# Moving eight modulation chunks of the second layer into the first layer's second attention

## The chip, the cores and the metric

The kernel runs on one core of one Trainium2 chip. The metric is the time of one execution on the device in microseconds, as the median of several runs. A profiled execution gives the trace that is read here. Engines are named as in the profile: PE is TensorE (PEld its weight loads), DVE is VectorE, ACT is ScalarE, POOL is GpSimd, SP is SyncE, whose queue (SPq) issues the weight loads.

## What is computed

The reference is a backbone of two layers (`DEPTH = 2`) over 256 latent tokens and 256 context tokens of width 1024, all in float32. Cut to what matters here:

```
for l in range(DEPTH):
    mod  = sc  @ w_mod[l] + b_mod[l]            # six vectors of 1024 for the latent tokens
    modc = scc @ w_mod[l] + b_mod[l]            # and six for the context tokens
    sh1, s1, g1, sh2, s2, g2 = split(mod)
    h = modulate(x, norm1_g[l], sh1, s1)        # needs vectors 0 and 1 (chunks 0 to 3)
    y, yc = token_mixers(h, hc, ...)            # conformer, Hyena, two attentions, gates, w_out
    x = x + g1 * y                              # vector 2 (chunks 4 and 5)
    h2 = modulate(x, norm2_g[l], sh2, s2)       # vectors 3 and 4 (chunks 6 to 9)
    x = x + g2 * hier_moe(h2, ...)              # vector 5 (chunks 10 and 11); 16 experts
```

`sc` and `scc` come from the conditioning vectors alone, so the modulation of the second layer can be computed at any time. In the second layer the context tokens are only keys and values, so most of its steps handle half as many tokens.

## The kernel before, in words

**The order.** The whole program is a list of steps written by hand in `layer_order` (L256): each is a pair of an engine (T for PE, V for DVE, S for ACT, P for POOL) and a name such as `("gate", l, branch, j)`. Every engine runs its own steps strictly in the order of the list and waits by semaphores for what a step needs. `spread` (L178) lays one list of groups evenly among another; `settled` (L192) moves the attention's output products behind the next gate step.

**A modulation chunk** (`mod_steps`, L208) is 512 of the 6144 columns of `w_mod`, and four steps: `mod` on PE (L1011 to L1021, matmuls on L1019, reading a chunk of 2 MB from the weight ring), `modrow` on ACT (L1541, a copy out of PSUM), `modT` on PE (transposes, L1025) and `modcol` on DVE (L2035, a sum and the bias). There are twelve chunks for each layer. For the second layer, chunks 0 to 3 are computed in the first layer's first attention (`ahead`, L342), chunks 4 and 5 at the layer boundary (L389 to L391) and chunks 6 to 11 between the projections of the second layer (L281 to L288, `mods`).

**The ring of weights.** All weights but those of the odd experts go through three places of 2 MB (`RING = 3`). `plan_ring` (L426) walks the chunks in the order in which PE first uses them and gives each the place whose present chunk is last used earliest. SP (L890 to L976) issues the loads in that same order on one queue: for each it waits until the last step that reads the place's earlier chunk is done, then issues the load. A load that waits holds back all loads behind it.

**Around the first layer's second attention (attention C).** `gate_groups(0, False)` is eight pairs of a `gate` step (L1059, 16 matmul records) and a `br` step (L1157), laid between the scores (`sC`, L1186), the transposes of the weights (`pTC`, L1193) and the outputs (`yC`, L1229). Gates 0 to 3 read chunk `("win", 0, 6)`, gates 4 to 7 `("win", 0, 7)`, the eight `br` steps `("wbr", 0, 0)`. Then come the gates of branch 2, which read `("win", 0, 10)`, `("wbr", 0, 2)` and `("win", 0, 11)`.

**The boundary of the layers.** The experts of the first layer end on PE (L1357); ACT stores the last rows to `y_dram` (L1774 to L1778); POOL gathers each token's two results (L1876) once the stores have landed and PE and ACT have ended their expert steps (L1866 to L1872); `mix` (L1248, L1249) adds them on PE, DVE gates them and adds them to `x` (L2579, L2583), then norm and `hT` (L1040) lead to the second layer's projections. At L963 to L965 SP waits for the last gather before it loads `("win", 1, 0)`, the second layer's first projection weights.

**The second layer's projections** on PE in order, with the chunks 6 to 11 (`mod`, then `modT` one or two steps later) between them: four `zD` and six `zB` (L1059), `zC` 0 and 1 (L1069), `vxT` (L1125), `zC` 2, four `dft` (L1131), `lnmean` (L1117), `zC` 3, `lnvar`, two `idft` (L1141), and `zAq`, `zAk` (L1069). Beside them DVE runs the convolutions in its own order: `cfconv` (L2112), `hyconv` (L2089 to L2093), `vx`, then `xc` (L2147) behind `lnmean` and `spec` (L2173 to L2178), for which `idft` waits.

Of the kernel before, what the change touches and what calls it, by code (L numbers as in the profile page):

```python
# [28 lines left out]
DEPTH = 2  # L29
# [108 lines left out]
def live(l):  # L138

    return TILES if l < DEPTH - 1 else 2  # L140


def with_side(l):

    return live(l) == TILES
# [32 lines left out]
def spread(main, side):  # L178

    out, n = [], 0  # L180
    for i, g in enumerate(main):
        upto = (i + 1) * len(side) // len(main)
        out += [g] + side[n:upto]
        n = upto
    return out
# [6 lines left out]
def settled(groups):  # L192

    groups, i = list(groups), 1
    while i < len(groups):
        kinds = [g[0][1][0] for g in groups]
        if kinds[i] in ("yA", "yC") and kinds[i - 1] in ("pTA", "pTC"):
            j = i + 1
            while j < len(groups) and kinds[j] not in ("gate", "br", "pTA", "pTC", "yM"):
                j += 1  # L200
            if j < len(groups) and kinds[j] in ("gate", "br"):
                groups.insert(j, groups.pop(i))
                i = j
        i += 1
    return [s for g in groups for s in g]


def mod_steps(l, chunks):  # L208
    out = []
    for c in chunks:  # L210
        out += [("T", ("mod", l, c)), ("S", ("modrow", l, c))]
        out += [("T", ("modT", l, c)), ("V", ("modcol", l, c))]
    return out
# [13 lines left out]
def filter_groups(l):  # L227

    net = [[("T", ("hf", l, n)), ("V", ("hfarg", l, n)), ("S", ("hfsin", l, n))] for n in (1, 2, 3)]
    net += [[("T", ("hf4", l, i)), ("V", ("hfwin", l, i)), ("S", ("hfsq", l, i))] for i in range(2)]  # L230
    spectrum = [[("T", ("fnorm", l)), ("V", ("fnorms", l))]]
    spectrum += [[("T", ("fdft", l, m)), ("S", ("fdftout", l, m))] for m in range(4)]
    return net, spectrum


def norm_steps(l, n, tiles):

    out = [("S", ("sq", l, n, t)) for t in tiles]
    out += [("V", ("rstd", l, n, tiles[0], tiles[-1] + 1))]
    out += [("V", ("scale", l, n, t)) for t in tiles]  # L240
    return out


def modulated_half(l, n, half):

    out = [("V", ("modfin", l, n, half))]
    for k in range(4 * half, 4 * half + 4):
        out += [("T", ("hT", l, n, k)), ("V" if k % 2 else "S", ("hTout", l, n, k))]
    return out


def modulated_steps(l, n):
    return modulated_half(l, n, 0) + modulated_half(l, n, 1)


def layer_order(l):  # L256

    tt = live(l)
    mods = [mod_steps(l, [c]) for c in range(4, 12)]
    pads = [("V", ("pads", l)), ("S", ("lamexp", l)), ("V", ("lam", l))]  # L260
    if l == 0:
        net, spectrum = filter_groups(l)
        first = [mod_steps(l, [c]) for c in range(4)]
        squares, normed = norm_steps(l, 1, range(TILES))[:TILES], norm_steps(l, 1, range(TILES))[TILES:]
        o = pads + net[0] + first[0][:2] + net[1] + first[0][2:] + squares[:2] + net[2] + squares[2:] + normed
        o += first[2][:2] + net[3] + first[2][2:] + modulated_half(l, 1, 0) + net[4]
        o += [("T", ("zD", l, 2))] + first[1][:2] + [("T", ("zD", l, 0))] + spectrum[0] + first[1][2:]
        o += [("T", ("zD", l, 3))] + first[3][:2] + spectrum[1] + [("T", ("zD", l, 1))] + spectrum[2] + first[3][2:]
        o += modulated_half(l, 1, 1) + spectrum[3] + spectrum[4]
    else:  # L270
        o = norm_steps(l, 1, range(TILES)) + modulated_steps(l, 1) + pads
        mods[:2] = [], []

    zd = {j: [("T", ("zD" if l else "zDrest", l, j)), ("S" if j >= 2 else "V", ("zDout", l, j))] for j in range(4)}
    zb = [[("T", ("zB", l, j)), ("S", ("zBout", l, j))] for j in range(6)]
# [18 lines left out]
    def gate_groups(bi, first):  # L294
        out = []
        for j in range(KD):
            out += [[("T", ("gate", l, bi, j)), ("S", ("gtanh", l, bi, j))],
                    [("T", ("br", l, bi, j)), ("V", ("gmul", l, bi, j))]
                    + ([] if first else [("P", ("gadd", l, bi, j))])]
        return out  # L300
# [17 lines left out]
    def attention(b):  # L318
        units = [(t, h) for t in range(tt) for h in HEADS_OF[b]]
        groups, turn = [], []  # L320
        for i in range(len(units) + 2):
            group = []
            if i < len(units) and i % 2 == 0:
                group += [("T", ("s" + b, l, t, h, n)) for t, h in units[i:i + 2] for n in range(2 if b == "A" else 1)]
            if i < len(units):
                group += [("V", ("mx" + b, l, *units[i])), ("S", ("ex" + b, l, *units[i]))]
            if 1 <= i <= len(units):
                group += [("V", ("p" + b, l, *units[i - 1]))]
            groups += [group] if group else []
            if i >= 2:  # L330
                t, h = units[i - 2]
                groups += turn[:1]
                turn = turn[1:]
                groups += [[("T", ("pT" + b, l, t, h)), ("S", ("pTout" + b, l, t, h))]]
                if h == 3 and b == "C":
                    groups += [[("T", ("yC", l, t)), ("S", ("yToutC", l, t))]]
                elif h == 3:
                    groups += [[("T", ("yA", l, t)), ("S", ("ysqA", l, t))]]
                    turn = [[("T", ("yM", l, t)), ("V", ("yrA", l, t))], [("T", ("yR", l, t)), ("V", ("ynA", l, t))]]
        return groups + turn  # L340

    ahead = []  # L342
    for c in range(4 if l + 1 < DEPTH else 0):
        steps = mod_steps(l + 1, [c])
# [5 lines left out]
    ropes = [[("V", ("rsC", l))]] + [g for g in prepared("C") if g[0][0] == "V"]  # L350
    o += settled(spread(conformer[12:] + spread(gate_groups(1, False), ahead),
                        units[:half] + spread(units[half:], ropes) + turns))
    o += settled(spread(gate_groups(0, False), attention("C")))
    net, spectrum = filter_groups(l + 1) if l + 1 < DEPTH else ([], [])

    o += merge(gate_groups(2, False), net)
# [29 lines left out]
    o += [("V", ("rows", l))]  # L386
    o += [("T", ("experts", l)), ("S", ("experts", l)), ("V", ("experts", l)), ("P", ("experts", l))]
    o += [("V", ("diag", l))] if with_side(l) else []
    if l + 1 < DEPTH:  # L389
        one, two = mod_steps(l + 1, [4]), mod_steps(l + 1, [5])  # L390
        o += one[:2] + two[:2] + one[2:] + two[2:]  # L391
    for t in range(tt):
        for hf in range(2):
            o += [("T", ("mix", l, t, hf))] if with_side(l) else []
# [24 lines left out]


ORDER = [("S", ("silu", 0))] + [s for l in range(DEPTH) for s in layer_order(l)]
STEPS = {e: [n for x, n in ORDER if x == e] for e in "TVSP"}
COUNT = {e: {n: i + 1 for i, n in enumerate(STEPS[e])} for e in "TVSP"}
# [106 lines left out]
def build_trunk(nc, xin, ccol, const, cols, rows, hfw, wr, wmod, win, wbr, wout, w1, w3, w2, out):  # L530
    with ExitStack() as ctx:
# [3 lines left out]
        def sem(name):  # L535
            return ctx.enter_context(nc.semaphore(name))
# [215 lines left out]
        y_gathered = [sem(f"y_gathered{t}") for t in range(TILES)]  # L752
# [96 lines left out]
        def _(sp):  # L849
# [40 lines left out]
            for i, (name, _) in enumerate(CHUNKS):  # L890
# [10 lines left out]
                if name[0] in experts_weights:  # L901
                    l = name[1]
# [57 lines left out]
                                    sp.wait_ge(more_stored[l], b * (16 * NE) + e * 16 + 16)  # L960
                                sp.sem_inc(waited, 1)
                    continue
                if name == ("win", 1, 0):  # L963

                    sp.wait_ge(y_gathered[live(0) - 1], 32)  # L965
                src = source[name[0]][name[1], name[2]]
                width = src.shape[1]
                if name[0] == "win" and name[2] in (2, 3):
# [1717 lines left out]
```

## Time and profile before

| | |
|---|---|
| median of 3 runs | 1601.78 us (1601.4 to 1606.16) |
| the profiled execution, its own time | 1604.79 us |
| its span in the trace | 1603.1 us |
| PE busy | 1491.4 us (93%) |
| DVE, ACT, POOL busy | 598.5, 288.9, 93.4 us |
| mean granted clock of TensorE | 0.972 of full speed |
| moved by DMA | 354.53 MB, 221 GB/s in the mean |

The profiled execution lies 3 us above the median. Times in the rows are microseconds from the start of the span. A timeline row gives start, length, engine, line, operation, what it writes and reads, and in brackets how long the engine stood idle before it and what released it. Records of successive matmuls overlap by some 0.15 us, so what a step takes of PE is read from the start of one row to the start of the next.

### The profile page before, as it was taken

To read this page: it belongs to the slowest core of one execution; us is meant where nothing else is said; L and a number is where in the kernel's file an instruction comes from. 1 tells how busy PE (TensorE), PEld (TensorE's weight loads), DVE (VectorE), ACT (ScalarE), POOL (GpSimd) and SP (SyncE) were. 2 spreads that over 40 slices of the span, in tenths; PEclk is the share of its full clock that TensorE was granted. 3 is DMA by queue.
4 is the path that set the end of the run, shared out by engine and by line. 5 is a ranking of instruction groups with operands and counts; after the bars stand their busy time and mean duration, and the time that the engine had idled before them with its cause. 6 is when DMAs were issued, how large, how long until landed. Compare 5 with 4: busy or idle time off the path is not lost.

```text
span 1603.1 us, 17603 instructions
## 1 busy us (share of the span) xinstructions
PE 1491.4 (93%) x6666; PEld 748.4 (47%) x6666; DVE 598.5 (37%) x1502; ACT 288.9 (18%) x596; POOL 93.4 (6%) x107
## 2 busy tenths in 40 slices
PE   5999999997999999799999997999989997999987
PEld 2544554443444444533333324755767874433332
DVE  4277633566532222512122124653665314211101
ACT  3211111332232301311111112110232302000000
POOL 0000010000101100000000001001001110000000
PEclk8999999999999999899999998999989998999999
DMA  9347321241312132499999966473232347899995
GB/s 370 137 173 272 132 78 53 80 150 61 131 53 83 53 157 73 165 350 407 415 408 411 412 244 236 177 280 138 89 131 79 132 185 299 332 424 421 424 422 207
DMA packets 38178, 354.53 MB, mean 221 GB/s; under 512 B 4272, under 2 KB 4656, under 8 KB 16976
## 3 DMA queue, kind: packets, MB, share of 16 engines
q1 hardware_dynamic: 30784, 329.73, 52.0%
q0 software_dynamic: 4016, 14.24, 2.4%
q10 hardware_dynamic: 3296, 9.44, 1.5%
q8 instruction: 55, 0.90, 0.2%
q14 instruction: 27, 0.22, 0.0%
HBM read 342.83 MB, written 10.56 MB: 220 GB/s over the span
## 4 chain that ended last, share of the span: by engine, by line
PE 62%; DVE 5%; DMA 4%; ACT 2%; issue 1%; SPq 1%; POOL 0%; DVEq 0%; PEldq 0%; ACTq 0%; POOLq 0%
PE ps L1347 18%; PE ps L1059 16%; PE ps L1357 5%; PE ps L1240 5%; PE ps L1157 3%; PE ps L1069 3%; DMA gates<-w 2%; PE ps L1369 1%; PE ps L1040 1%; DMA mr<-w 1%; PE ps L1019 1%; PE ps L1193 1%; PE ps L1335 1%; PE ps L1186 1%; PE ps L1229 1%
## 5 line engine op out<-in xcount | busy, mean ns | idle before, releaser
L1059 PE MATMUL ps<-hT,ring 128*128 128x512 f32 (+1 forms) x1344 | 452.6, 491 | 1.5 <-DVE hT L2071 1.5
L1059 PEld LDWEIGHTS ps<-hT,ring 128*128 128x128 f32 x1344 | 254.8, 192 | 177.3 <-issue 154.6
L1347 PE MATMUL ps<-ring,m 128*64 128x512 f32 x528 | 239.2, 604 | 9.7 <-DMA n_<-w 3.8
L1347 PEld LDWEIGHTS ps<-ring,m 128*64 128x64 f32 x528 | 70.0, 139 | 159.0 <-issue 150.3
L1069 PE MATMUL ps<-ring,hT 128*128 128x512 f32 (+1 forms) x352 | 126.0, 516 | 3.6 <-DMA ring<-win 3.6
L1157 PE MATMUL ps<-yT,ring 128*128 128x512 f32 (+1 forms) x256 | 96.0, 498 | 4.5 <-ACT n_ L1675 4.5
L1069 PEld LDWEIGHTS ps<-ring,hT 128*128 128x128 f32 x352 | 66.4, 190 | 62.3 <-issue 58.1
L1240 PE MATMUL ps<-ring,wide 128*128 128x512 f32 x192 | 83.1, 593 | 0.8 <-POOL wide L1822 0.8
L1349 PE MATMUL ps<-n_,m 128*64 128x512 f32 x176 | 82.0, 621 | 0.0
L1634 ACT ACTIVATE gates<-ps,hbg 128x512 f32<-128x512 f32 (+1 forms) x64 | 37.2, 581 | 247.7 <-PE ps L1059 185.2
L1349 PE MATMUL ps<-wide,m 128*64 128x512 f32 x176 | 79.6, 598 | 0.0
L2202 DVE SCALAR_TENSOR_TENSOR gates<-gates,ps 128x512 f32<-128x512 f32 (+1 forms) x48 | 26.6, 555 | 140.5 <-PE ps L1157 115.8
L1349 PE MATMUL ps<-hT,m 128*64 128x512 f32 x176 | 77.8, 595 | 0.0
L2112 DVE SCALAR_TENSOR_TENSOR n_<-n_,col 128x512 f32<-128x512 f32 (+1 forms) x120 | 74.2, 619 | 4.3
L1822 POOL TENSOR_TENSOR wide<-wide,gates 128x512 f32<-128x512 f32 (+1 forms) x48 | 48.0, 1000 | 419.7 <-DVE gates L2202 419.7
L2449 DVE SCALAR_TENSOR_TENSOR m<-m,ps 128x512 f32<-128x512 f32 x16 | 11.0, 688 | 144.1 <-ACT m L1744 144.1
L1157 PEld LDWEIGHTS ps<-yT,ring 128*128 128x128 f32 x256 | 46.7, 194 | 33.9 <-issue 23.2
L1019 PE MATMUL ps<-ring,cc 128*32 128x512 f32 x384 | 50.8, 652 | 12.1 <-DMA ring<-wmod 9.6
L1357 PE MATMUL ps<-ring,yT 128*32 128x512 f32 x256 | 58.1, 595 | 0.0
L1240 PEld LDWEIGHTS ps<-ring,wide 128*128 128x128 f32 x192 | 36.2, 190 | 45.5 <-issue 45.5
L1349 PE MATMUL ps<-ring,m 128*64 128x512 f32 x128 | 56.4, 595 | 0.0
L2462 DVE TENSOR_TENSOR m<-m,ps 128x512 f32<-128x512 f32 x16 | 11.0, 687 | 105.9 <-PE ps L1349 105.9
(362 smaller groups left out, 1769.1 us busy)
## 6 DMA issues: line engine op xcount, KB each, us to landing
ring<-w SPq DMA_DIRECT2D x40, 2048.0 KB, 10.8
ring<-wmod SPq DMA_DIRECT2D x24, 2048.0 KB, 8.5
ring<-win SPq DMA_DIRECT2D x24, 2048.0 KB, 8.1
n_<-w SPq DMA_DIRECT2D x13, 2048.0 KB, 14.7
hT<-w SPq DMA_DIRECT2D x13, 2048.0 KB, 17.7
wide<-w SPq DMA_DIRECT2D x13, 2048.0 KB, 15.6
ring<-wbr SPq DMA_DIRECT2D x8, 1024.0 KB, 4.8
ring<-wout SPq DMA_DIRECT2D x4, 2048.0 KB, 7.9
```

The costliest lines, as they stand in the source:

```text
L1019: last = pe.matmul(b[g:g + 32, :], cc[:, 32 * k:32 * k + 32], w[:, k, :], start=(k < 4), stop=(k >= 4), skip_group_check=True)
L1059: last = pe.matmul(b[:, 0:W], w[:, k, jj * P:(jj + 1) * P], hT[:, k, 0:W], start=(k == 0), stop=(k == KD - 1))
L1069: last = pe.matmul(b[:, 0:wid], hT[:, k, t * P:(t + 1) * P], w[:, k, 0:wid], start=(k == 0), stop=(k == KD - 1))
L1157: last = pe.matmul(b[:, 0:W], w[:, k, j * P:(j + 1) * P], yT[:, bi in (1, 2), k, 0:W], start=(k == 0), stop=(k == 1))
L1240: last = pe.matmul(b, acc[:, k, t * P:(t + 1) * P], w[:, k, :], start=(k == 0), stop=(k == KD - 1))
L1347: pe.matmul(ps[0:HALF, bnk, :], left[:, k, 0:HALF], even[k], start=(k == 0), stop=(k == n_k - 1), skip_group_check=True)
L1349: last = pe.matmul(ps[HALF:P, bnk, :], left[:, k, HALF:P], odd[k], start=(k == 0), stop=(k == n_k - 1), skip_group_check=True)
L1357: last = pe.matmul(ps[SIDE * g:SIDE * (g + 1), bnk, :], left[:, k0 + k, rows_:rows_ + SIDE], weights[:, k0 + k, cols_], start=(k == 0), st ...
L1634: last = act.activation(gth[:, g % 2, 0:W], bank(("gate", l, bi, j))[:, 0:W], ACT.Tanh, bias=hbg[:, bi * 8 + j:bi * 8 + j + 1], scale=0.5)
L1822: last = nc.gpsimd.tensor_tensor(acc[:, j, 0:W], acc[:, j, 0:W], gtmp[:, g % 2, 0:W], ALU.add)
L2112: last = v.scalar_tensor_tensor(out=o, in0=ud[:, j, 0:ns, k:k + 256], scalar=w(k), in1=o, op0=ALU.mult, op1=ALU.add)
L2202: last = v.scalar_tensor_tensor(out=dst, in0=gth[:, g % 2, 0:W], scalar=1.0, in1=bank(("br", l, bi, j))[:, 0:W], op0=ALU.add, op1=ALU.mult)
```

## The change

The change alters only the order. Chunks 4 to 11 of the second layer's modulation are all computed in the first layer's attention C, spread one to each gate pair; the two at the boundary and the six among the second layer's projections go away there. Their number and their content stay. SP's wait for the last gather ahead of `("win", 1, 0)` is removed, so that this load is issued as soon as its place is free.

```diff
@@ layer_order
         o = norm_steps(l, 1, range(TILES)) + modulated_steps(l, 1) + pads
-        mods[:2] = [], []
+        mods = [[]] * 8
@@
-    o += settled(spread(gate_groups(0, False), attention("C")))
+    later = []
+    for c in (4, 5, 6, 7, 8, 9, 10, 11) if l + 1 < DEPTH else ():
+        steps = mod_steps(l + 1, [c])
+        later += [steps[:2], steps[2:]]
+    o += settled(spread(spread(gate_groups(0, False), later), attention("C")))
@@
     o += [("V", ("diag", l))] if with_side(l) else []
-    if l + 1 < DEPTH:
-        one, two = mod_steps(l + 1, [4]), mod_steps(l + 1, [5])
-        o += one[:2] + two[:2] + one[2:] + two[2:]
@@ block.sync
                     continue
-                if name == ("win", 1, 0):
-
-                    sp.wait_ge(y_gathered[live(0) - 1], 32)
                 src = source[name[0]][name[1], name[2]]
```

Since `plan_ring` is computed from the order, the places and the order of the loads change with it. By its rule, place 1 carries the eight modulation chunks of attention C one after the other, place 2 holds `("wbr", 0, 0)` until the eighth `br` step, and place 0 holds first `("win", 0, 6)` until gate 3, then `("win", 0, 7)` until gate 7, then `("win", 0, 10)`. Before, `("win", 0, 7)` had a place since the end of branch 1 and `("win", 0, 10)` took its place after gate 3. After the experts the next three loads are `("win", 1, 0)`, `("win", 1, 1)` and `("win", 1, 2)` (1 MB), each behind the last reader of `w1`, `w3` and `w2`.

## Rows read from the trace of the kernel before

**Rows 1.** The page: the span and the first line of section 1.
```profile
span 1603.1 us, 17603 instructions
...
PE 1491.4 (93%) x6666; PEld 748.4 (47%) x6666; DVE 598.5 (37%) x1502; ACT 288.9 (18%) x596; POOL 93.4 (6%) x107
```

**Rows 2.** Windows: attention C; length, busy PE, PEld, DVE, ACT, POOL, clock, DMA, GB/s.
```profile
415.17:505.44 90.27, 88.30 (x339) 42.06 (x337) 36.64 (x113) 29.10 (x77) 11.10 (x9) 1.00 0.17 61
```

**Rows 3.** Timeline of PE, second layer's projections, 1000 to 1081 us.
```profile
1000.11 31.32 PE L1059 MATMUL ps<-hT,ring 128*128 128x256 f32 x144 [1.25 <-DVE hT L2071]
1031.36 1.92 PE L1019 MATMUL ps<-ring,cc 128*32 128x512 f32 x16
...
1042.88 7.11 PE L1069 MATMUL ps<-ring,hT 128*128 128x512 f32 x16 [3.65 <-DMA ring<-win]
1049.82 0.60 PE L1025 MATMUL ps<-con,mr 128*128 128x128 f32 x4
1050.35 1.92 PE L1019 MATMUL ps<-ring,cc 128*32 128x512 f32 x16
1052.20 7.13 PE L1069 MATMUL ps<-ring,hT 128*128 128x512 f32 x16
...
1080.79 3.69 PE L1141 MATMUL ps<-con,m 128*128 128x256 f32 x16 [1.02 <-DVE m L2178]
```

**Rows 4.** Timeline of PE, first layer's attention C.
```profile
427.39 0.63 PE L1193 MATMUL ps<-con,n_ 128*128 128x128 f32 x4 [1.15 <-ACT esk L1679]
...
457.96 0.60 PE L1193 MATMUL ps<-con,m 128*128 128x128 f32 x4
...
461.38 7.03 PE L1059 MATMUL ps<-hT,ring 128*128 128x512 f32 x16
...
501.05 0.38 PE L1193 MATMUL ps<-con,n_ 128*128 128x128 f32 x2
...
505.44 4.99 PE L1059 MATMUL ps<-hT,ring 128*128 128x512 f32 x11
```

**Rows 5.** Timeline of SP's queue, same stretch; the second load's issue ends the row.
```profile
413.62 44.86 SPq L970 DMA_DIRECT2D ring<-win  x2
```

**Rows 6.** Issues in 458 to 459 us (alone), 976.9 to 977.4 (second of three): us to landing last.
```profile
ring<-win SPq DMA_DIRECT2D x1, 2048.0 KB, 8.0
...
ring<-win SPq DMA_DIRECT2D x1, 2048.0 KB, 12.6
```

**Rows 7.** Timeline of DVE, second layer's projections.
```profile
1036.24 0.48 DVE L2093 SCALAR_TENSOR_TENSOR m<-m,col 128x256 f32<-128x256 f32 x1
...
1060.31 8.30 DVE L2112 SCALAR_TENSOR_TENSOR n_<-n_,col 128x256 f32<-128x256 f32 x16
...
1075.12 0.75 DVE L2147 TENSOR_TENSOR n_<-n_,ps 128x256 f32<-128x256 f32 x2 [2.52 <-PE ps L1117]
```

**Rows 8.** Timeline of PE at the boundary of the layers.
```profile
958.27 5.34 PE L1019 MATMUL ps<-ring,cc 128*32 128x512 f32 x32 [2.54 <-issue]
...
968.08 1.10 PE L1248 MATMUL ps<-wide,n_ 128*128 128x512 f32 x2 [2.99 <-DMA hT<-y_scratch,m]
```

**Rows 9.** Timeline of SP's queue at the boundary.
```profile
932.66 10.93 SPq L970 DMA_DIRECT2D ring<-wmod  x2
```

**Rows 10.** Timeline of POOL at the boundary: the first gather.
```profile
961.36 0.94 POOL L1876 DMA_INDIRECT wide<-y_scratch,m  x1 [83.87 <-PE ps L1019]
```

**Rows 11.** Timeline of ACT's queue at the boundary: the last store.
```profile
957.04 0.62 ACTq L1778 DMA_DIRECT2D y_scratch<-gates  x1
```

**Rows 12.** Issues of ACT's last stores, 955.7 to 958 us, and one pair earlier, 922.3 to 928.
```profile
y_scratch<-gates ACTq DMA_DIRECT2D x2, 128.0 KB, 2.4
...
y_scratch<-gates ACTq DMA_DIRECT2D x2, 128.0 KB, 9.2
```

**Rows 13.** Windows at the boundary, columns as in rows 2: the mixing of the tiles.
```profile
968.10:973.30 5.20, 5.20 (x9) 2.18 (x10) 0.69 (x1) 0.00 (x0) 2.28 (x3) 0.67 0.96 355
973.30:983.75 10.45, 10.45 (x25) 4.36 (x23) 7.82 (x9) 3.44 (x6) 0.00 (x0) 1.00 0.81 309
```

## The prediction

> **What bounds the kernel now.** I read the page first: PE is busy for 93% of the span [rows 1]. So the first question for every moved step is whether PE has room where it leaves and where it arrives. The windows by stage answer that for the place of arrival: in attention C of the first layer PE is busy for 88.30 of 90.27 us at full clock, while DMA is at 0.17 and DVE and ACT are busy less than half of the time [rows 2]. PE sets the end there, and the free resource (DMA) is not the one that ends anything. The timelines of PE then show the places of departure. Among the second layer's projections PE runs without a pause but for two waits, 3.65 us for a weight load that queued behind modulation chunks and 1.02 us for DVE [rows 3]. At the boundary of the layers PE is not the bound: it runs the two modulation chunks in a pause, is done with them before 965.1 us and then waits 2.99 us more for the gathered rows [rows 8]. The chain there is store, gather, mix.
>
> The number of chunks does not change. So the change can gain only from waits that go, and loses what was hidden at the boundary.
>
> **Price of a chunk.** Start to start, a `modT` takes 1050.35 - 1049.82 = 0.53 us and a `mod` 1052.20 - 1050.35 = 1.85 us of PE [rows 3], 2.38 us together. ACT adds one copy and DVE two short sums, both on engines with room.
>
> **Part 1, attention C gains eight chunks.** 8 x 2.38 = 19.0 us of PE. The wait of 1.15 us ahead of the first `pTC` [rows 4] is for ACT's and DVE's chain and does not depend on the new steps, while `mod` 4 and `modT` 4 now stand ahead of it: it is filled, -1.15 us. A second pause of 0.82 us ahead of the last `yC` lies within the stretch that is priced next.
>
> New waits come from the ring. Between gate 3 and gate 4 place 0 must be reloaded. Gate 3 ends at 457.96 and gate 4 starts at 461.38, 3.42 us of other steps [rows 4]; with `mod` 7 and `modT` 7 it is 5.8 us. The trace of before has a load that is released by this very gate: it is issued at 413.62 + 44.86 - 0.33 = 458.15 [rows 5], 0.2 us behind the gate, and lands 8.0 us later [rows 6]. A wait for a load ends some 0.1 us after landing. So gate 4 waits 8.3 - 5.8 = 2.5 us. In the same way `("win", 0, 10)` is now released by gate 7: 501.05 to 505.44 are 4.39 us of other steps [rows 4], 6.8 us with a chunk, so the first gate of branch 2 waits 8.3 - 6.8 = 1.5 us. The load behind each (the next modulation chunk, `wbr`) stands later in the same queue; of three loads issued together the second landed 12.6 us after its issue, 4.6 us more than the lone load's 8.0 [rows 6], so it can take little from the first. I leave up to 1 us each for it in the range. The modulation chunks themselves are in time: between the end of one `mod` and the next there are at least a gate of 6.9 us and some 3.5 us of other steps, 10.4 us, against 8.3 us for a load.
>
> Sum: 19.0 - 1.15 + 2.5 + 1.5 = **+21.9 us**, from 17.0 (neither ring wait, both pauses filled) to 24.
>
> **Part 2, the second layer's projections lose six chunks.** From 1000.11 to the first `idft` at 1080.79 are 80.7 us [rows 3]. Without 6 x 2.38 = 14.3 us of chunks and the two waits (4.7 us) PE's own work is 61.7 us, so PE could be there at 1061.8. What is late next is DVE. It ends the fourth `hyconv` at 1036.7 [rows 7], before any chunk has held it up; then come a `cfconv` of 15 steps, two `hyconv` and `vx`, and a `cfconv` of 16 steps in 8.30 us [rows 7]: 7.8 + 3.7 + 8.3, to 1056.5. `lnmean` takes about 1.2 us until `xc` can start, and from the start of `xc` to `idft` it was 1080.79 - 1075.12 = 5.7 us [rows 3, 7]. PE reaches `lnmean` at about 1056.9, so `idft` starts at 1063.8 or so. The projection weights are in time: `("win", 1, 5)` now follows the last `zD` at 1014 and is needed at 1035. Gain **-17.0 us**, from -16 to -18.9 (PE alone).
>
> **Part 3, the boundary.** Taking `mod` 4 and 5 out of it gains nothing: they end before the rows are there [rows 8]. The loads at 932.66 and 943.26 [rows 9] become `("win", 1, 0)` and `("win", 1, 1)`, 2 MB for 2 MB. The third, `("win", 1, 2)` of 1 MB, is new in this place: it used to be issued behind the gathers and is now released when the last expert product ends at 955.7 [rows 8]. ACT issues the last of its stores at 957.04, and the gather, at 961.36, waits for them [rows 10, 11]. The last two took 2.4 us in an idle DMA and 9.2 us in the pair before, where some 4 MB of loads ran beside them [rows 12]. A quarter of that load, a quarter of the excess: (9.2 - 2.4) / 4 = 1.7 us later; the ends are 0 and 6.8 us. That the projection weights are there 30 us earlier buys nothing, since PE waited for DVE and not for them at 1000.11 [rows 3].
>
> The two chunks also kept PE at work ahead of the mixing. Before, the clock was 0.67 in the mean while the first tile was mixed, which took 5.2 us against 10.45 / 3 = 3.5 us for each of the others at 1.00 [rows 13]. Now PE is idle from 955.7 to nearly 970 and starts at the lower level (1.2 GHz), so I add 0.6 us, from 0 to 1.7 (twice the loss seen). The Trainium skill, TensorE: Matmul & The Clock Gate, section Why this matters for your kernels, speaks against this part: idle gaps between bursts bring the lower clock back. The trace agrees in kind, by the 0.67 behind a pause of 3 us; if the rule costs a second stretch of the same length, this term is 1.7 and the sum 8.3. The Trainium skill, DMA: Bandwidth & Descriptors, section Queues, rings and completion order, says that each DMA engine alternates between the queues that have work, packet by packet. By that rule the stores wait for no more than the 1 MB load itself, half of the 4.6 us that 2 MB more took in [rows 6]: 2.3 us in place of 1.7, and the sum 7.8.
>
> Sum: **+2.3 us**, from 0 to 8.5.
>
> **Total**: 21.9 - 17.0 + 2.3 = +7.2 us. The profiled execution (1604.79 us) would become 1612.0. Against the median of the runs, 1601.78, it is **1609.0 us**. About 0.3% (4.8 us) is what a measurement of this kernel can tell from no change.
>
> **Rivals.**
> - *No new wait.* The ring waits and the store's delay don't appear, for example because the steps between the gates stretch by themselves. For it speaks that both waits are short against their cover; against it, that the 8.0 us is measured on the very load. Then 19.0 - 1.15 - 17.0 + 0.6 = +1.5 us: 1603.3 us, not slower. It decides if gate 4 starts less than 0.5 us behind its predecessor.
> - *The gather starts earlier.* The trace names PE's modulation matmuls as what released POOL's first gather at 961.36 [rows 10]. If they really hold it up, it could start when the stores have landed, 957.04 + 2.4 = 959.4 [rows 11, 12] and a reaction, up to 1.9 us earlier. With no ring wait, both pauses filled and the projections at PE's own speed: 17.0 - 18.9 - 1.9 = -3.8 us, 1598.0, and beyond 0.3% with a little more. Against it: the code makes the gather wait for the experts alone, and PE's list has the chunks behind them. This is the one way to a faster kernel.
> - *Coupled queues.* ACT now waits in `modrow` for a `mod` that stands behind a gate, DVE in `modcol` for `modT`; softmax steps are queued behind both. If each chunk costs PE one more pause like the 1.15 us of [rows 4], it is 7.2 + 8 x 1.15 = +16.4: 1618 us. For it: the order in each engine is strict. Against it: DVE and ACT are under half busy [rows 2], and the scores' chains have a gate of 6.9 us to catch up.
>
> **How the numbers follow.** Forecast case 0.58, no new wait 0.24, earlier gather 0.07, coupled queues 0.11. The forecast case reaches from about +3 to +12 us; a little of it lies within 0.3%. So faster 0.07, same 0.30, slower 0.63. The range goes from 1599, which takes in the case without waits and half of the one with the early gather, to 1616, which takes in the forecast's upper bounds and leaves most of the coupled case out.
>
> **What would show it.** In the profile after: 16 x 8 records of L1019 within 415 to 530 us; a wait of PE on `ring<-win` of 2 to 3.5 us ahead of the fifth gate and of 1 to 2.5 us ahead of the first gate of branch 2; gate 2,0 some 22 us later; the stretch from the first `zD` to `idft` 17 us shorter, `idft` still behind DVE's L2178; the first gather 5 to 7.5 us behind the end of L1357, where it was 5.6; the clock at 0.5 in the first mixing. The prediction is wrong if PE meets no load wait in attention C, if the second layer gains more than 19 us, or if the mixing starts earlier than before against the end of the experts.

## The result and the profile after

The changed kernel takes 1614.54 us in the median of 6 runs (1612.35 to 1618.31), the kernel before, beside it, 1605.57 us (1601.4 to 1608.7). The ratio is 1.0061, 95% interval 1.0046 to 1.0076: **slower by some 9.7 us** (the interval is 7.4 to 12.2 us), where the prediction had +7.2 us. The profiled execution takes 1614.24 us with a span of 1612.5 us; before it was 1604.79 and 1603.1.

The page of the kernel after, span and first line of section 1, answers [rows 1]:

```profile
span 1612.5 us, 17602 instructions
...
PE 1491.7 (93%) x6666; PEld 749.5 (46%) x6666; DVE 601.7 (37%) x1502; ACT 288.9 (18%) x596; POOL 93.6 (6%) x107
```

PE does the same 6666 matmuls in the same 1491 us. What was added is time in which PE waits, and the place of the chunks has moved. I cut both traces at the same marks and subtract:

| stretch | before | after | difference | predicted |
|---|---|---|---|---|
| start to gate 0,0 | 415.17 | 414.33 | -0.8 | 0 |
| gate 0,0 to gate 2,0 (attention C) | 90.27 | 112.30 | **+22.0** | +21.9 |
| gate 2,0 to the first output product | 75.27 | 75.25 | 0.0 | 0 |
| to the first expert product (router) | 96.71 | 98.63 | +1.9 | 0 |
| experts | 278.30 | 278.30 | 0.0 | 0 |
| end of experts to the first gather | 5.64 | 8.35 | +2.7 | +1.7 |
| gather to the first `zD` | 38.75 | 39.52 | +0.8 | +0.6 |
| first `zD` to `idft` | 80.68 | 63.47 | **-17.2** | -17.0 |
| `idft` to the end | 522.31 | 522.35 | 0.0 | 0 |

**Attention C.** Windows of the kernel after from gate 0,0 to gate 2,0, columns as in [rows 2]; then its timeline of PE around gate 4 and the first gate of branch 2, which answer [rows 4]:

```profile
414.33:526.63 112.30, 107.48 (x498) 49.03 (x497) 42.80 (x129) 34.27 (x86) 11.14 (x9) 1.00 0.52 197
```

```profile
468.43 0.60 PE L1023 MATMUL ps<-con,mr 128*128 128x128 f32 x4
471.13 7.11 PE L1057 MATMUL ps<-hT,ring 128*128 128x512 f32 x16 [2.10 <-issue]
...
523.44 1.09 PE L1227 MATMUL ps<-n_,m 128*64 128x128 f32 x16 [0.62 <-ACT n_ L1683]
526.63 7.10 PE L1057 MATMUL ps<-hT,ring 128*128 128x512 f32 x16 [2.10 <-issue]
```

PE's busy time rose by 107.48 - 88.30 = 19.2 us, 2.40 us a chunk. The rest of the 22.0 is waits: 2.10 us twice ahead of a gate, and the 1.15 us of [rows 4] is gone. "issue" in the brackets says only that the view found no event. The queue tells what it was. SP's timeline of the kernel after, and two answers about issues (463 to 466 us, 517.5 to 518.3 us; size, us to landing):

```profile
463.35 0.33 SPq L968 DMA_DIRECT2D ring<-win  x1
465.67 41.58 SPq L968 DMA_DIRECT2D ring<-wmod  x4
517.99 0.33 SPq L968 DMA_DIRECT2D ring<-win  x1
```

```profile
ring<-win SPq DMA_DIRECT2D x1, 2048.0 KB, 7.7
...
ring<-win SPq DMA_DIRECT2D x1, 2048.0 KB, 8.6
```

463.35 + 7.7 = 471.05, and gate 4 starts at 471.13; 517.99 + 8.6 = 526.59, and the gate starts at 526.63. Each load is issued as soon as the last reader of its place (gate 3, gate 7) is done and is waited for to its landing.

**The boundary.** POOL's first gather, PE's first mixing product and the window of the first tile in the kernel after (they answer [rows 10], [rows 8] and [rows 13]), then the issues of ACT's last stores (979.2 to 981 us, answers [rows 12]) and of the load beside them (978.6 to 979.3 us):

```profile
987.16 0.94 POOL L1874 DMA_INDIRECT wide<-y_scratch,m  x1 [86.58 <-issue]
```

```profile
993.74 2.04 PE L1246 MATMUL ps<-wide,n_ 128*128 128x512 f32 x2 [14.93 <-DMA hT<-y_scratch,m]
```

```profile
993.74:999.90 6.16, 6.16 (x8) 2.62 (x9) 0.69 (x1) 0.00 (x0) 2.45 (x3) 0.56 0.99 368
```

```profile
y_scratch<-gates ACTq DMA_DIRECT2D x2, 128.0 KB, 4.9
...
ring<-win SPq DMA_DIRECT2D x1, 1024.0 KB, 5.4
```

The stores land after 4.9 us where it was 2.4, and the gather starts 8.35 us behind the experts where it was 5.64. The first tile is mixed at a clock of 0.56 in the mean (before 0.67) and takes 6.16 us in place of 5.20.

**The second layer's projections.** Timeline of PE, kernel after, answers the last row of [rows 3]:

```profile
1083.27 1.10 PE L1115 MATMUL ps<-n_,con 128*128 128x256 f32 x4 [0.74 <-DVE n_ L2110]
...
1090.15 3.69 PE L1139 MATMUL ps<-con,m 128*128 128x256 f32 x16 [1.46 <-DVE m L2176]
```

The wait for weights at `zC` is gone; PE now meets DVE twice, at `lnmean` and at `idft`.

### The profile page after: what moved, and what is told of

Read it like the earlier page. It is cut to its first block, busy times and chain, and to the rows that moved or that the text cites. A ratio compares the mean times of both kernels' runs of the same rounds, so it can differ in the third digit from the quotient of the medians.

```text
span 1612.5 us, 17602 instructions
## 1 busy us (share of the span) xinstructions
PE 1491.7 (93%) x6666; PEld 749.5 (46%) x6666; DVE 601.7 (37%) x1502; ACT 288.9 (18%) x596; POOL 93.6 (6%) x107
## 4 chain that ended last, share of the span: by engine, by line
PE 60%; DVE 7%; DMA 4%; issue 2%; ACT 2%; SPq 1%; POOL 0%; POOLq 0%; PEldq 0%; ACTq 0%; DVEq 0%
PE ps L1345 18%; PE ps L1057 14%; PE ps L1355 5%; PE ps L1238 5%; PE ps L1155 3%; DMA gates<-w 2%; DVE n_ L2110 2%; PE ps L1067 2%; PE ps L1367 1%; DMA mr<-w 1%; PE ps L1038 1%; PE ps L1017 1%; PE ps L1191 1%; PE ps L1333 1%; PE ps L1184 1%
```

## The experiments

My theory: the change loses by two separate waits that its new order of loads makes, at gates in attention C and at the boundary, beside chunks that cost PE 2.4 us each wherever PE is the bound. The rivals: the chunks' own queueing costs more than PE's time; the idle PE ahead of the mixing costs clock.

### Putting SP's wait back, and keeping PE at work

```diff
  # e1, in block.sync of the kernel after
+ if name == ("win", 1, 0):
+     sp.wait_ge(y_gathered[live(0) - 1], 32)
  # e4, e1 and in the mixing
+ if t == 0 and half == 0:
+     for _ in range(7):
+         pe.matmul(b, ident, dft_c[:, 0, :], start=True, stop=True)
```

> The changed kernel with SP's wait for the last gather ahead of the second layer's first projection load put back, and nothing else. Theory (the 1 MB load that was let loose slows ACT's last two stores, and the gather waits for these): the stores take 2.4 us again in place of 4.9, the first gather starts 5.6 us behind the experts' last matmul in place of 8.3, and the whole is 2.5 to 2.7 us shorter than the changed kernel, about 6.5 us above the kernel before. The first tile is still mixed in about 6.2 us, since PE is idle ahead of it as in the changed kernel. Rival (the gather is late because the two chunks are gone, not because of the load): the gather stays at 8.3 us and the time at that of the changed kernel. Rival (the early load pays in the projections): the first projection waits for weights, and the kernel gets slower than the changed one.

> The first of these kernels (the changed one with SP's wait put back) with seven matmuls of 512 columns ahead of the first mixing, on data that is in place, into the bank that the mixing overwrites: they compute nothing that is used and keep PE at work while it waits for the gathers. Theory (the first tile is slow because PE starts at its lower clock level): the granted clock is at full from the start of the mixing, the first tile takes about 3.5 us in place of 6.2, total 2 to 2.6 us below the first kernel. Rival (the first tile is slow because the gathered rows land one tile after the other): it stays at about 6 us, whatever the clock says, and so does the total.

The first took 1611.65 us, ratio to before 1.0050 (1.0032 to 1.0069), 0.0011 or 1.8 us less than the kernel after where 2.5 to 2.7 were expected; the second 1612.94, 1.0057 (1.0036 to 1.0078), no shorter than the first. Both intervals overlap that of the kernel after, so the times alone settle nothing. The traces do. POOL's timeline with the wait put back:

```profile
986.21 0.94 POOL L1876 DMA_INDIRECT wide<-y_scratch,m  x1 [83.87 <-issue]
```

The experts end at 980.58 there, so the gather is back at 5.63 us behind them: the 1 MB load was what held the stores, though PE was as idle as in the kernel after. But this execution gave the gain back elsewhere. Windows of the same kernel behind its wait of 2.28 us for the load of branch 2, and of the kernel after behind the like wait:

```profile
528.18:532.00 3.82, 3.82 (x6) 1.66 (x7) 0.00 (x0) 0.00 (x0) 0.00 (x0) 0.66 1.06 320
```

```profile
526.63:530.00 3.37, 3.37 (x8) 1.60 (x9) 0.00 (x0) 0.00 (x0) 0.00 (x0) 1.00 1.08 309
```

The same gate, nearly the same wait, once at 0.66 and once at full clock: that gate took 8.80 us against 7.10. The transposes ahead of the first `zD` took 11.37 us in place of 10.07 as well, behind a like pause.

With seven products of no use ahead of the mixing, PE's timeline is:

```profile
983.05 7.94 PE L1247 MATMUL ps<-con 128*128 128x512 f32 x14 [2.26 <-DVEq L2566]
992.98 1.10 PE L1251 MATMUL ps<-wide,n_ 128*128 128x512 f32 x2 [1.99 <-DMA hT<-y_scratch,m]
993.91 1.46 PE L1252 MATMUL ps<-hT,n_ 128*128 128x512 f32 x2
995.16 1.92 PE L1251 MATMUL ps<-wide,n_ 128*128 128x512 f32 x2
```

The first product runs at full clock (1.10 us, not 2.04), and two rows later they are slow again (1.92): behind the pause of 1.99 us the clock fell during the work. The stretch from the first mixing product to `hT` is 21.88 us, as in the kernel before (21.89); it is 22.18 in the first of these kernels and 22.87 in the kernel after. So the extra products took back what the idle PE had added, 0.3 us against the first kernel and 1.0 us against the profile after. My expectation of 2 to 2.6 us was wrong: I had expected the first tile in 3.5 us, and it took 5.20, as in the kernel before. The slow products that the kernel before has too are still there, behind one more pause.

### Chunks at gates where the ring has time

```diff
  # e2, in the kernel after: chunk behind gate j of a branch
- o += settled(spread(spread(gate_groups(0, False), later), attention("C")))
+ o += settled(spread(with_chunks(gate_groups(0, False), {0: 4, 1: 5, 2: 6, 4: 7, 5: 8, 6: 9}), attention("C")))
- o += merge(gate_groups(2, False), net)
+ o += merge(with_chunks(gate_groups(2, False), {4: 10, 6: 11}), net)
```

> The changed kernel with the same eight chunks on other gates: chunks 4, 5, 6 at gates 0, 1, 2 and 7, 8, 9 at gates 4, 5, 6 of the second attention, 10 and 11 at gates 4 and 6 of the branch behind it. By the ring's rule the gate weights then get a place early. Theory (the two waits of 2.1 us of PE are the price of the place): both go, no other load wait comes, the stretch from the first gate of attention C to the output projection is 4.2 us shorter than in the changed kernel, total some 4 us below it. Rival (the ring only moves its wait, since eight loads of 2 MB still go through one place): waits of PE on wmod chunks of the same sum appear, no change in time.

1608.17 us, ratio 1.0028 (1.0019 to 1.0038), clear of the kernel after's interval: 0.0033, or 5.3 us, where about 4 were expected for the ring's waits. In this kernel's trace SP issues the load for gate 4 at 452.85 us and the gate starts at 466.75: the load has 13.9 us, where the kernel after gave it 5.7. One window holds the difference, from gate 0,0 to the first output product; before in the first fence, this kernel in the second:

```profile
415.17:580.71 165.54, 163.57 (x524) 74.99 (x523) 52.72 (x143) 45.19 (x97) 21.23 (x17) 1.00 0.18 67
```

```profile
414.75:597.33 182.58, 181.96 (x684) 81.81 (x683) 58.60 (x159) 49.92 (x105) 21.22 (x17) 1.00 0.42 154
```

Eight chunks add 18.4 us of busy PE, and since most of the pauses of before are filled, 17.0 us to the stretch (kernel after: 22.0). Of these 5.0 us, 4.2 are the two waits. The loads, not the queueing of the chunks' steps on ACT and DVE, made the difference. DMA's share rose from 0.18 to 0.42, and PE waited for no load: it stood idle for 0.62 us in all.

### Both mended

```diff
  # e10: e2 with SP's wait for the last gather ahead of ("win", 1, 0), as in e1
```

> The kernel after with both of its new waits avoided: chunks at the places of the ring-friendly kernel, and SP's wait for the last gather put back. Theory (the two are the only losses of the change beside what the chunks cost PE): attention C and branch 2 +17.0 us as in the ring-friendly kernel, boundary 0, projections -17.2: within 1 us of before, ratio 0.999 to 1.001. Rival (losing PE's work ahead of the mixing costs clock at each of the next stretches): +2 to +3 us.

1605.65 us, ratio 1.0003 (0.9989 to 1.0017): no difference from before. The steps add up: 1.0061 for the change, 1.0028 without the ring's waits, 1.0003 without the load at the boundary too. The stretches are +17.0, 0 (gather 5.64 us behind the experts) and -17.2 us. So the ring's waits (some 5 us) and the load beside the stores (some 4 us by the ratios, 2.7 us of it seen at the gather) account for the loss, within an interval that reaches from -1.8 to +2.7 us. The rival with the clock (+2 to +3 us) is not needed for it, and only the interval's upper end would leave it room.

### SP's wait alone

```diff
  # e7, in the kernel before
- if name == ("win", 1, 0):
-     sp.wait_ge(y_gathered[live(0) - 1], 32)
```

> Kernel before with nothing changed but SP's wait for the last gather, taken away. The load of (win, 1, 0), 2 MB, now goes out at 955.7 beside ACT's last stores, and (win, 1, 1) and (win, 1, 2) behind the two chunks, beside the gathers. Theory (loads beside the stores set the gather's start and nothing is gained, since the projections waited for DVE and not for their weights): first gather 8 to 9.5 us behind the end of the experts in place of 5.6, the tiles' rows another 0 to 3 us later by the loads beside the gathers, +2.5 to +6 us in all. Rival (the delay in the kernel after came from the chunks that no longer stand there): gather at 5.6 us and within 1 us of before.

1613.79 us, ratio 1.0049 (1.0031 to 1.0067), **7.9 us** slower by one wait removed, a little more than I expected. SP's queue, the issues of the stores and the load in 955.7 to 958.2 us, and POOL's first gather:

```profile
956.20 8.20 SPq L967 DMA_DIRECT2D ring<-win  x3
```

```profile
ring<-win SPq DMA_DIRECT2D x1, 2048.0 KB, 8.9
y_scratch<-gates ACTq DMA_DIRECT2D x2, 128.0 KB, 7.6
```

```profile
967.39 0.94 POOL L1873 DMA_INDIRECT wide<-y_scratch,m  x1 [89.48 <-issue]
```

The stores take 7.6 us beside a load of 2 MB, 4.9 beside one of 1 MB (kernel after) and 2.4 with none [rows 12]; the gather starts 11.25, 8.35 and 5.64 us behind the experts. The gather follows the stores nearly one for one (+5.2 and +5.6 us, +2.5 and +2.7), and each MB in front of them costs about 2.6 us. In this kernel the next 2 MB load was issued some 5 us behind the first, before the stores had landed, so a part of the 5.2 us can be its share. In this trace another 1.4 us lie between the first gather and the mixing, beside the loads that follow, and 3.2 in the projections, most of them in one product stretch at a low clock (last section). The wait that SP had in the kernel before was thus worth its place: it kept the queue away from a small transfer on the chain. It also shows that the late gather needs no missing chunks: here both stand at the boundary.

### Two chunks alone

```diff
  # e3, in the kernel before: chunks 4 and 5 leave the boundary for attention C
+ for c in (4, 5) ...: later += [steps[:2], steps[2:]]
+ o += settled(spread(spread(gate_groups(0, False), later), attention("C")))
- o += one[:2] + two[:2] + one[2:] + two[2:]
```

> The kernel before with chunks 4 and 5 alone moved from the boundary into the second attention; the six in the second layer's projections stay, and SP's wait stays. Theory (the two were hidden behind the stores and gathers at the boundary, and cost PE's full price where they go): attention C is 2 x 2.38 = 4.8 us longer, the boundary is not shorter but about 1 us longer (the first tile mixed in about 6.2 us at the lower clock, where it took 5.2), the projections stay at 80.7 us from the first zD to idft: 5.8 us above the kernel before. Rival (the two stood on the boundary's chain, as the trace's releaser of the first gather says): the gather starts up to 1.9 us earlier against the experts' end, and the total is 2 to 3 us above the kernel before.

1613.85 us, ratio 1.0063 (1.0042 to 1.0084): some 10 us, more than the 5.8 expected. The rival is out: the first gather starts 5.66 us behind the experts, and before it was 5.64. The boundary itself got no longer, since from the experts' end to `hT` are 34.2 us as before; the expected 1 us for the clock came to 0.25 in the mixing. Attention C to the first output product is 8.1 us longer, of which 4.8 are PE's. PE's timeline of this kernel at the end of the attention, and its window:

```profile
508.66 0.52 PE L1194 MATMUL ps<-con,n_ 128*128 128x128 f32 x2 [1.94 <-DVE n_ L2279]
509.80 1.98 PE L1230 MATMUL ps<-n_,m 128*64 128x128 f32 x16 [0.62 <-ACT n_ L1686]
511.70 9.08 PE L1060 MATMUL ps<-hT,ring 128*128 128x512 f32 x16
```

```profile
510.00:515.00 5.00, 5.00 (x20) 2.89 (x19) 0.00 (x0) 0.38 (x1) 0.00 (x0) 0.50 0.83 347
```

The even spreading put a new pause of 1.94 us behind DVE ahead of the last weights' transposes, and behind it PE ran at half speed: the sixteen products took 1.98 us in place of 1.09, the gate 9.08 in place of 7.1. These two rows are 2.9 us. The cause of the pause stands in the timelines of ACT and then DVE of this kernel:

```profile
504.21 0.69 ACT L1635 ACTIVATE gates<-ps,hbg 128x512 f32<-128x512 f32 x1 [5.12 <-PE ps L1060]
504.93 0.47 ACT L1676 ACTIVATE n_<-ps,nm 128x256 f32<-128x256 f32 x1
...
507.38 1.13 DVE L2279 TENSOR_SCALAR n_<-n_,rden 128x256 f32<-128x256 f32 x1
```

The last softmax's exponential (L1676) had its input at 499.5 us, but stands in ACT's list behind the activation of a gate that PE ends only at 504.1. In the kernel before it stood ahead of that activation (494.92 against 501.30). The two chunks shifted it there, because `spread` counts them as groups. This is akin to the rival "coupled queues" of the prediction, but not the same: the softmax waits behind a gate and not behind `modrow` or `modcol`. The order of the change does not have it. Another 0.9, 1.2 and 1.3 us lie in the router, the transposes and the projections, each behind a pause that the kernel before has too; whether they belong to the edit I can't tell from one trace.

### The chunks in the second layer's own attention

```diff
  # e5, in the kernel before
  # (only the changed parts of the lines)
+ mods = [[]] * 8      # second layer; with_chunks lays chunks of the layer itself behind gates
+ with_chunks(conformer[12:], {0: 6}) + spread(with_chunks(gate_groups(1, False), {0: 7, 1: 8, 4: 9, 5: 10}), ahead)
+ with_chunks(gate_groups(0, False), {1: 11})
  # e6: 6 between the squares and the scaling of the norm behind the mixing, 7 to 11 in the attention;
  #     SP waits for the last gather ahead of ("wmod", 1, 6)
+ o = normed[:TILES] + six[:2] + normed[TILES:] + six[2:] + modulated_steps(l, 1) + pads
```

> Kernel before, chunks 4 and 5 stay at the boundary, chunks 6 to 11 leave the second layer's projections for the second layer's own attention (one in the conformer's gates, four in branch 1, one in branch 0), where PE of the kernel before stands idle 1.22, 2.00, 4.50, 2.92 and 0.84 us at five places. Theory (the departure is worth 17.2 us, as the kernel after showed, and what decides is whether PE has pauses at the place of arrival): -17.2 + 6 x 2.38 = -2.9 us, less the pauses that are filled, between 4 and 9 us: -7 to -12 us against before, 1591 to 1597 us. Rival (the pauses are chains that start behind the chunk, so that they stay as long): -3 us against before. Rival (new ring waits of some 2 us each, as in the kernel after): 0 to +3 us.

> As the last, but chunk 6 stands in PE's pause of 6.2 us between the mixing and the first transposes of the second layer, its load issued behind the last gather; 7 to 11 in the conformer's first gate and branch 1. Theory (a chunk in a pause longer than itself costs nothing): another 1 to 2.4 us below the last kernel. Rival (its 2 MB load or its matmuls push the gathered rows or the norm's steps back, or it arrives too late): equal or some 2 us above the last kernel.

The first took 1609.01 us, ratio 1.0026 (1.0013 to 1.0039): slower, where I had expected a gain of 7 to 12 us. The departure was worth -17.2 us again, but `idft` to the output products grew from 230.17 to 250.21 us. The windows of that stretch, before and this kernel:

```profile
1080.79:1310.96 230.17, 215.60 (x1033) 168.46 (x1033) 104.44 (x290) 53.39 (x125) 23.64 (x34) 0.96 0.30 111
```

```profile
1062.90:1313.11 250.21, 229.93 (x1153) 172.35 (x1153) 106.05 (x300) 56.97 (x131) 23.56 (x34) 0.96 0.41 152
```

PE's work rose by 14.3 us, exactly six chunks, and its idle time did not fall but rose, from 14.6 to 20.3 us. Two rows of PE of this kernel show the first of the reasons, and one shows the second:

```profile
1155.06 2.43 PE L1028 MATMUL ps<-ring,cc 128*32 128x512 f32 x16 [2.39 <-DMA ring<-wmod]
...
1182.85 0.69 PE L1228 MATMUL ps<-con,n_ 128*128 128x128 f32 x2 [5.45 <-ACT n_ L1684]
1196.80 3.20 PE L1028 MATMUL ps<-ring,cc 128*32 128x512 f32 x16 [3.25 <-DMA ring<-wmod]
```

Gates of the second layer take 3.6 us and not 7. SP issued these two loads at 1146.87 and 1188.83 us, each as a gate ended (1146.84 and 1188.80), and they took some 8 us; only 5 to 6 us of steps lie between that and the chunk. That makes 5.6 us of new waits. The five pauses that I had counted on sum to 11.3 us where they were 11.5, and the longest (4.50 us) is there with 5.45. Rows of DVE and ACT of this kernel show why:

```profile
1169.62 1.42 DVE L2252 TENSOR_REDUCE mx<-ps 128x1 f32<-128x512 f32 x2 [5.20 <-PE ps L1187]
1181.34 0.69 ACT L1684 ACTIVATE n_<-ps,nm 128x512 f32<-128x512 f32 x1 [4.25 <-DVE nm L2253]
```

From the maximum of one pair of scores (the first row) to the exponential of the next (the second), DVE works without a break through softmax steps and small steps of a normalisation. That takes 11.7 us, and in the kernel before 11.9. This chain starts with PE's scores (L1187), and the chunk (1166.49) stands ahead of them, so the chain and the pause only move. My sum had taken a pause for free room without asking what it waits for. Of the two rivals that I had named, both held: the pauses stayed, and new ring waits came.

The second took 1606.01 us, ratio 1.0004 (0.9993 to 1.0015), 0.0022 or 3.5 us less than the first, where 1 to 2.4 were expected. Its chunk 6 on PE:

```profile
985.59 1.92 PE L1029 MATMUL ps<-ring,cc 128*32 128x512 f32 x16 [0.48 <-DMA ring<-wmod]
989.19 0.63 PE L1035 MATMUL ps<-con,mr 128*128 128x128 f32 x4 [1.67 <-ACT mr L1553]
991.33 8.93 PE L1050 MATMUL ps<-n_,x 128*128 128x128 f32 x64 [1.51 <-DVE n_ L2074]
```

From the first mixing product to `hT` are 21.88 us, before 21.89. There a chunk is free. The other five still cost 17.2 us from `idft` to the output products, with 5.8 us of waits for their loads, and that uses up what their departure gives.

### Each chunk where it was cheapest

```diff
  # e9, in the kernel before: 4 and 5 stay, 6 behind the mixing as in e6,
  # 7 behind lnmean in the second layer, 8 to 11 at gates 0, 1, 2, 4 of attention C
+ mods = [[]] * 7 + [mod_steps(l, [7])]
+ o += row_of[7] * (l > 0) + zc_[3] + col_of[7]
+ with_chunks(gate_groups(0, False), {0: 8, 1: 9, 2: 10, 4: 11})
```

> Each chunk where a stretch of the runs so far was cheapest for it. 4 and 5 at the boundary as before (no cost), 6 in PE's pause behind the mixing (no cost in the run that had it there), 7 in the second layer behind lnmean, where PE waits 1.46 us for DVE ahead of the first idft (2.38 - 1.46 = 0.9 us), 8 to 11 at gates 0, 1, 2 and 4 of attention C (4 x 2.38 - 1.15 = 8.4 us, no ring wait at the like places of the run that avoided them). Theory (costs of places add up): 8.4 + 0.9 - 17.2 = -7.9 us against before, 1594 to 1598 us. Rival (the clock behind PE's pauses differs by some us from execution to execution and hides it, or a load in the second layer comes late): -2 to -5 us. Rival (a chunk costs what the attention of the second layer showed, over 3 us each): 0 or above.

1598.40 us in the median of 9 runs (1594.63 to 1600.03) against 1605.37, ratio **0.9955 (0.9941 to 0.9969)**: 7.2 us faster than before (7.9 expected) and some 17 us faster than the kernel after. By stretches: to the first output product +9.6 us (8.4 expected; the first pause kept 0.83 us and one of 0.76 stands ahead of an output product), `zD` to `idft` -16.4 (-16.3 expected); what else differs from the first trace of before (router +1.4, `hT` to `zD` +1.4, `idft` to the output products -2.4) lies behind pauses, but for the first gather, which starts 6.15 us behind the experts and not 5.64. PE's timeline at chunk 7:

```profile
1070.44 1.92 PE L1030 MATMUL ps<-ring,cc 128*32 128x512 f32 x16
1072.29 3.72 PE L1080 MATMUL ps<-ring,hT 128*128 128x256 f32 x16
1075.85 0.60 PE L1036 MATMUL ps<-con,mr 128*128 128x128 f32 x4
1076.29 1.03 PE L1128 MATMUL ps<-n_,con 128*128 128x256 f32 x4
1077.15 3.62 PE L1152 MATMUL ps<-con,m 128*128 128x256 f32 x16
```

The 1.46 us for DVE ahead of `idft` are gone; the chunk stands in their place and costs 0.9 us.

### The kernel before once more

> The kernel before, unchanged, for a second trace. Theory (the clock that PE is granted behind a pause of some us is not fixed by the kernel, and the router's stretch, the transposes and the first projection differ by 0 to 2 us each from one execution to the next): stretches between marks agree within 0.2 us except those that begin behind a pause, which differ by 0.3 to 2 us. Rival (these stretches are set by the kernel's own order): all within 0.2 us.

An execution of 1602.7 us. The marks agree within 0.2 us in nearly all stretches; `zD` to `idft` is 0.5 us shorter, by a shorter wait for the weights at `zC`. Two stretches differ by much more, the router's with +1.5 us (98.20, 1.4 of it in the products of L1289 behind a pause of 2.5 us) and `idft` to the output products with -2.9 us (227.29). Timeline of PE in the latter, the kernel before and the second execution of it:

```profile
1177.43 3.62 PE L1204 MATMUL ps<-n_,m 128*64 128x128 f32 x32 [2.00 <-ACT n_ L1685]
```

```profile
1178.32 1.97 PE L1204 MATMUL ps<-n_,m 128*64 128x128 f32 x32 [1.90 <-ACT n_ L1685]
```

The same instruction behind nearly the same pause, once at the lower clock and once at the upper. It makes 1.65 of the 2.9 us. So a difference of 1 to 3 us behind a pause in a single trace is no evidence for or against an edit.

## Why the prediction was right

The prediction (+7.2 us, range 1599 to 1616, slower the likeliest) held, and its forecast case was the one that happened. The absolute figure came out less well: 1609.0 us was forecast and 1614.54 measured, but 3.8 of these 5.5 us are the base, whose median was 1601.78 us in the three runs known then and 1605.57 in the six beside the kernel after. Step by step:

- **Price of a chunk**, 2.38 us: PE's busy time gives 2.40 in attention C and 2.39 in the second layer's attention.
- **Part 1**, +21.9 us: +22.0. Its parts are less exact than the sum. Gate 4 waited 2.10 us (2.5 predicted), the first gate of branch 2 waited 2.10 (1.5 predicted, because the load took 8.6 us to land and not 8.0), the pause ahead of the first `pTC` was filled as said. The row of one load, [rows 6], and the row of the steps between two gates, [rows 4], were enough.
- **Part 2**, -17.0 us: -17.2. DVE's chain set the end as worked out, at `lnmean` (0.74 us) and `idft` (1.46 us). Counting the chunks alone (14.3 us) would have missed 2.9 us.
- **Part 3**, +2.3 us: +3.5 in the trace; by the ratios it is about 4 between the kernel with friendlier gates and the one with both mended (1.0028, 1.0003), and 1.8 by the kernel with the wait put back. The mechanism was right, the size was not: the gather is 8.35 us behind the experts, outside the 5 to 7.5 I had named. The stores' term was 1.7 and measured 2.5 us: I took the excess in proportion to the bytes beside them, from a pair with 4 MB of loads. The runs with 1 and 2 MB in front give 2.5 and 5.2 us. The Trainium skill, DMA: Bandwidth & Descriptors, section Queues, rings and completion order, has the DMA engines alternate between queues by packet; the 2.3 us that I had worked out by it beside the sum lies nearer to the 2.5. That is one number and not a proof of the rule: the 2.3 was meant as a ceiling, and the same working gives 4.6 us beside 2 MB, where 5.2 were measured. No run separates alternation from a plain sharing by bytes. The clock term was 0.6 and measured 1.0 (22.87 against 21.89 us from the first mixing product to `hT`). That size is luck in part: in the five other kernels where PE stood idle for 10 us or more ahead of the mixing it was 0.25 to 0.67 us.
- **The clock.** The Trainium skill, TensorE: Matmul & The Clock Gate, section Why this matters for your kernels, has idle gaps bring the lower clock back. The trace agrees (0.56 in the first tile), but the case in which that costs a second stretch of the same length did not come.
- **What was missing**: +1.9 us in the router's stretch, where no step had moved. The kernel before gave 96.71 and 98.20 us in two executions, and the traces of the experiments lie between 96.6 and 98.6. Most of it is the clock behind one pause: the 16 products of L1289 take 2.14 us behind a pause of 2.46 in the first trace of before, 3.56 in its second, and 3.57 in the kernel after, behind 2.45 each time. That is 1.4 us, and it is luck. The rest is some 0.4 us. The three highest stretches, 98.6, are all kernels with eight chunks moved, but two others with eight have 97.6, so whether the rest belongs to the change stays open.
- **The rivals.** No new wait: out, both waits stand in the trace. Gather starts earlier: out; with no chunk in front of it, it stays at 5.63 us behind the experts in the kernel with the wait put back and at 5.66 us in the two-chunk kernel, so PE's chunks never held it. The [rows 10] entry that names them as the releaser misled. Coupled queues: not in this change (22.0 against 21.9); the two-chunk kernel has a pause of a kindred sort.

## What to carry to other kernels

A step that is moved is priced at three places: what stood behind it where it leaves, PE's time and the free room where it arrives, and each load whose place comes free later by the new order; a load that is issued by its predecessor's last reader costs its whole landing time less the steps between. A pause is room for a step only if what PE waits for has already been started by then; the rows ahead of the pause tell that. And a wait in a load queue that looks like a brake may keep megabytes away from a small store on the chain: ask what is in flight at that time before it is taken away.

## What was not expected of the hardware

Behind a pause of about 2 us the clock that PE is granted is not fixed by the kernel. In two executions of the kernel before, the 16 products of L1289 took 2.14 and 3.56 us behind pauses of 2.46 and 2.45 us, and the 32 products of L1204 took 3.62 and 1.97 us behind pauses of 2.00 and 1.90 us. The transposes ahead of the first `zD` show it across kernels: from `hT` to `zD` it takes 10.06 to 10.25 us in five traces and 11.35 to 11.54 in five others, all behind the same pause of 6.2 us (the two kernels with a chunk in that pause have one of each). The largest difference is behind the wait at `zC`: 7.11 us behind 3.65 in the kernel before [rows 3], and in the kernel with SP's wait removed, whose code differs in that wait alone:

```profile
1052.32 10.16 PE L1066 MATMUL ps<-ring,hT 128*128 128x512 f32 x16 [3.83 <-DMA ring<-win]
```

So a pause that an edit adds can bring up to 3 us on top of its own length, differently from one execution to the next, and an edit that takes a pause away takes this draw too. It may be a part of the spread of the runs, which no run here separates: 20 runs of the kernel before on one chip went from 1599.98 to 1610.81 us. And the last two stores, 128 KB each, took 2.4, 4.9 and 7.6 us with 0, 1 and 2 MB issued on another queue 0.7 us ahead of the first of them: the delay grew in step with the bytes in front of them, at about half of these loads' own time to land (5.4 and 8.9 us).
